# Layer normalisation by token tiles, and products ordered to match, in a two-layer hybrid decoder on one core

## The reference

```
h = layer_norm(x, emb_ln_g, emb_ln_b)
for i in range(2):
    mix = hybrid_mixer(h, ...)                      # projections, attention, linear recurrence, @ w_out
    h = layer_norm(ALPHA * h + mix, ln1_g[i], ln1_b[i])
    ffn = peer_ffn(h, ...)                          # 16384 experts, 16 of them per token and head
    ple = sigmoid(h @ ple_gate_w[i]) * (p[i] @ ple_w[i])
    h = layer_norm(ALPHA * h + ffn + ple, ln2_g[i], ln2_b[i])

def layer_norm(x, g, b):                            # over the 1024 columns of a token
    mu = x.mean(-1); var = square(x - mu).mean(-1)
    return (x - mu) * rsqrt(var + 1e-5) * g + b
```

## Time and profile before

| | |
|---|---|
| median of 3 runs | 3377.86 us (3376.49 to 3378.57) |
| the profiled execution | 3379.62 us, span from first to last instruction 3377.8 us |
| TensorE busy | 3236.6 us (96%) |
| VectorE busy | 2538.5 us (75%) |
| Pool busy | 2055.1 us (61%) |
| ScalarE busy | 1386.4 us (41%) |
| mean granted TensorE clock | 0.987 of full speed |

### The profile page before, as it was taken

How to read it: one execution, slowest core, us unless ns; L and a number is a source line. 1 busy time by engine, 2 the same in 40 slices (tenths; PEclk the granted TensorE clock), 3 DMA queues, 4 the chain that set the end, 5 groups by cost and what they waited for, 6 DMA issues and landing times. The chain is left out here.

```text
span 3377.8 us, 47082 instructions
## 1 busy us (share of the span) xinstructions
PE 3236.6 (96%) x17370; PEld 2888.0 (86%) x17370; DVE 2538.5 (75%) x4654; ACT 1386.4 (41%) x2726; POOL 2055.1 (61%) x1388
## 2 busy tenths in 40 slices
PE   5999899999999999999989998999999999999996
PEld 4787689999999988888777876899999999888885
DVE  5965359886876588888877734698769656888887
ACT  1235013466666533333212531135666664333331
POOL 5931677666677655555479046766666776555552
PEclk9999899999999999999999999999999999999998
DMA  3210224687899999999623012256888999999994
GB/s 122 89 68 26 88 75 159 230 294 298 298 334 355 354 387 370 360 361 363 245 75 99 32 51 88 76 200 239 302 301 300 348 352 357 384 364 361 359 362 154
DMA packets 312676, 817.12 MB, mean 242 GB/s; under 512 B 22272, under 2 KB 119552, under 8 KB 309120
## 3 DMA queue, kind: packets, MB, share of 16 engines
q1 hardware_dynamic: 112256, 349.02, 29.8%
q0 software_dynamic: 73728, 268.47, 20.6%
q10 hardware_dynamic: 126464, 196.63, 16.6%
HBM read 712.84 MB, written 101.19 MB: 241 GB/s over the span
## 5 line engine op out<-in xcount | busy, mean ns | idle before, releaser
L1247 POOL TENSOR_TENSOR u_lo<-panel,u_hi 128x1024 fp32r<-128x1024 f32 x256 | 619.4, 2420 | 318.0 <-ACT u_hi L1052 314.5
L594 PE MATMUL ps<-hT_hi,u_lo 128*128 128x384 f32 x2048 | 700.3, 342 | 0.0
L594 PE MATMUL ps<-hT_lo,u_hi 128*128 128x384 f32 x2048 | 684.6, 334 | 0.0
L594 PE MATMUL ps<-hT_hi,u_hi 128*128 128x384 f32 x2048 | 684.5, 334 | 0.0
L594 PE MATMUL ps<-v_hi,w_lo 128*128 128x512 f32 x1536 | 597.7, 389 | 0.1
L594 PE MATMUL ps<-v_hi,w_hi 128*128 128x512 f32 x1536 | 597.5, 389 | 0.0
L594 PE MATMUL ps<-v_lo,w_hi 128*128 128x512 f32 x1536 | 597.5, 389 | 0.0
L1264 POOL TENSOR_TENSOR v_lo<-panel,v_hi 128x1024 fp32r<-128x1024 f32 x128 | 311.6, 2434 | 381.7 <-ACT v_hi L1114 381.6
L1199 POOL TENSOR_TENSOR ring_hi<-panel,cst 128x512 fp32r<-128x512 f32 x244 | 275.4, 1129 | 432.1 <-PE ps L574 254.6
L1114 ACT CAST v_hi<-panel 128x1024 fp32r<-128x1024 f32 x256 | 269.1, 1052 | 641.8 <-PE ps L594 637.9
L1052 ACT CAST u_hi<-panel 128x1024 fp32r<-128x1024 f32 x256 | 268.1, 1048 | 445.4 <-PE ps L594 442.5
(11 more groups left out here) (264 smaller groups left out, 5670.1 us busy)
## 6 DMA issues: line engine op xcount, KB each, us to landing
panel<-in_u SPq DMA_DIRECT2D x256, 512.0 KB
panel<-in_v SPq DMA_DIRECT2D x256, 512.0 KB
gate_scratch<-arena ACTq DMA_DIRECT2D x24, 2048.0 KB
act_scratch<-arena ACTq DMA_DIRECT2D x124, 384.0 KB
arena<-act_scratch ACTq DMA_DIRECT2D x62, 768.0 KB
arena<-gate_scratch ACTq DMA_DIRECT2D x62, 768.0 KB
panel<-in_w_in SPq DMA_DIRECT2D x28, 1024.0 KB, 5.2
panel<-in_wq SPq DMA_DIRECT2D x16, 1024.0 KB, 5.1
```

What stands on the lines that cost most here:

```text
L594: mm = nc.tensor.matmul(o, lhs[a], rhs[b_], start=(start and n == 0), stop=(stop and n == 2))
L1247: pr.mark(nc.gpsimd.tensor_tensor(u_lo[:, j % URING].rearrange("p c n -> p (c n)"), u_tile(j), u_hi[:, j % URING].rearrange("p c n -> p (c ...
```

## The change

Both normalisations go token tile by token tile, and the products ahead of them finish token tile by token tile:

- `project` of the output's second half does its first four chunks as before and its last four (all that the ring holds) with the token tile as outer loop.
- The second expert product does tiles 0 to 123 as before and the last `GROUP` of four with the token tile as outer loop, signalling `y_tile` after each.
- VectorE takes moments of the first half early (`moments`), and then, for each token tile, adds, takes moments and makes the variance (`tile_variance`, `summed_variance`), with a root of its own on ScalarE. Scaling is two operations instead of three: (h - mean) * g, then * rstd + b (`tile_scaled`), in an order that puts other tiles' variances between.
- Token tile 0's moments and first scaling read `acc0` in PSUM; its copy to h is gone. `ADDED` reaches 128 at tile 123 instead of 127.
- Pool splits the query weights (panels 9 and on) only after all four tiles of the first normalisation; in layer 1 TensorE's first transposition also waits for all additions of the layer before.
- SP sends the output as four transfers, one for each token tile.

```diff
-ADDED = [max(0, (tile_ - LATE_DOTS) * SLOTS // (NK - 1 - LATE_DOTS)) for tile_ in range(NK)]
+ADDED = [min(SLOTS, max(0, (tile_ - LATE_DOTS) * SLOTS // (NK - 1 - GROUP - LATE_DOTS))) for tile_ in range(NK)]
...
-                    for c in range(NC):
+                    for c in range(NC - RING if tiles_last else NC):
...
+                    if tiles_last:
+                        late = []
+                        for m in range(4):
+                            for c in range(NC - RING, NC):
+                                if m == 0:
+                                    late.append(next_chunk())
+                                    used[0] += 1
+                                mm = matmul3(o4[m], [x_[:, c, m * P:(m + 1) * P] for x_ in (hT_hi, hT_lo)],
+                                             late[c - NC + RING], False, c == NC - 1)
+                                if m == 3:
+                                    pr.mark(mm, ring_used)
+                            if m < 3:
+                                pr.mark(mm, products)
+
+
+                if layer > 0:
+                    pe.wait_ge(y_added.sem, layer * y_added.per_layer)
                 turn(h, G_T1, 0, -NT)
...
+                for i in range(3):
+                    for j in range(NK - GROUP, NK):
+                        if i == 0:
+                            need_v_lo(pr, j)
+                            pe.wait_ge(w_lo_ready.sem, layer * w_lo_ready.per_layer + j + 1)
+                        for half in range(2):
+                            mm = second(j, i, half)
+                        if i == 2:
+                            pr.mark(mm, y_done)
+                    if i < 2:
+                        pr.mark(mm, y_tile)
...
-                root(3, rstd[:])
+                for i in range(NT):
+                    root(3 + i, rstd[:, i:i + 1])
...
-                split_panels(7, len(MIXER_PANELS), 1, 2)
+                split_panels(7, 9, 1, 2)
+                pool.wait_ge(h_ready.sem, layer * h_ready.per_layer + h_ready.before + NT)
+                split_panels(9, len(MIXER_PANELS), 1, 2)
...
+                def tile_variance(i):
+
+                    mixed(4 + i)
+                    step(moments(4 + i))
+                    variance(i)
+
+                def variance(i):
+
+                    step(nc.vector.bn_aggr(mv[:, i, :], stat[:, i, :]))
+                    pr.mark(nc.vector.tensor_scalar(rstd[:, i:i + 1], mv[:, i, 1:2], LN_EPS, None, ALU.add), var_ready)
+
+                def tile_scaled(i, roots, src=None):
+
+                    pr.need(root_ready, roots)
+                    step(nc.vector.reciprocal(rstd[:, i:i + 1], rstd[:, i:i + 1]))
+                    ins = nc.vector.scalar_tensor_tensor(out=h[:, i, :], in0=h[:, i, :] if src is None else src,
+                                                         scalar=mv[:, i, 0:1], in1=lng[:, 0, :],
+                                                         op0=ALU.subtract, op1=ALU.mult)
+                    if src is None:
+                        step(ins)
+                    else:
+                        pr.link(ins, y_added)
+                    pr.mark(nc.vector.scalar_tensor_tensor(out=h[:, i, :], in0=h[:, i, :], scalar=rstd[:, i:i + 1],
+                                                           in1=lng[:, 1, :], op0=ALU.mult, op1=ALU.add), h_ready)
...
+                tile_variance(0)
+                tile_scaled(0, 3)
+                tile_variance(1)
+                tile_variance(2)
+                tile_scaled(1, 4)
+                tile_variance(3)
+                tile_scaled(2, 5)
+                tile_scaled(3, 6)
...
-                pr.mark(nc.vector.tensor_copy(h[:, 0, :], acc0), y_added)
...
+                def summed_variance(i):
+
+                    if i < 3:
+                        dve.wait_ge(y_tile.sem, layer * y_tile.per_layer + i)
+                    else:
+                        dve.wait_ge(y_done.sem, layer * y_done.per_layer + NK)
+                    for half in range(2):
+                        hh = h[:, i, half * 512:(half + 1) * 512]
+                        n = pr.mark(nc.vector.tensor_tensor(hh, hh, bank(2 * (i - 1) + half), ALU.add), y_added)
+                    pr.need(y_added, n)
+                    for half in range(2):
+                        last = nc.vector.bn_stats(stat[:, i, 6 * half:6 * half + 6], h[:, i, half * 512:(half + 1) * 512])
+                    step(last)
+                    variance(i)
+
+                row_variance()
                 dve.wait_ge(ln2_in.sem, layer * ln2_in.per_layer + 32)
-                norm(h, step, root, lambda ins: pr.mark(ins, h_ready))
+                tile_scaled(0, 7, acc0)
+                summed_variance(1)
+                tile_scaled(1, 8)
+                summed_variance(2)
+                summed_variance(3)
+                tile_scaled(2, 9)
+                tile_scaled(3, 10)
...
-            sp.dma_start(out.rearrange("(i p) d -> p i d", p=P), h[:]).then_inc(out_sent.sem, 16)
-            sp.wait_ge(out_sent.sem, 16)
+            for i in range(NT):
+                sp.wait_ge(h_ready.sem, DEPTH * 2 * NT + i + 1)
+                sp.dma_start(out[i * P:(i + 1) * P, :], h[:, i, :]).then_inc(out_sent.sem, 16)
+            sp.wait_ge(out_sent.sem, 16 * NT)
```

More of the change, by code:

```diff
@@ L777, in _ @@
                 for half in range(2):
-                    project(lambda i: take(G_OUT + 4 * half + i, (pre1, 4 * half + i + 1)), True, None if half else 1)
+                    project(lambda i: take(G_OUT + 4 * half + i, (pre1, 4 * half + i + 1)), True, None if half else 1,
+                            half == 1)
                 turn(h, G_T3, 2, 0)
@@ L857, in _, with second @@
                 pe.wait_ge(g_kept.sem, layer * g_kept.per_layer + NG)
-                for j in range(NK):
+                def second(j, i, half):
+                    return matmul3(bank(2 * i + half), [x_[:, j % GROUP, i * P:(i + 1) * P] for x_ in (w_hi, w_lo)],
+                                   [x_[:, j % VRING, half * 512:(half + 1) * 512] for x_ in (v_hi, v_lo)],
+                                   j == 0, j == NK - 1)
+                for j in range(NK - GROUP):
                     need_v_lo(pr, j)
@@ L865, in _ @@
                                        + max(u for u in range(NK) if ABANKS[u % 3] == k) + 1)
-                        mm = matmul3(bank(k), [x_[:, j % GROUP, i * P:(i + 1) * P] for x_ in (w_hi, w_lo)],
-                                     [x_[:, j % VRING, half * 512:(half + 1) * 512] for x_ in (v_hi, v_lo)],
-                                     j == 0, j == NK - 1)
+                        mm = second(j, i, half)
                     pr.mark(mm, y_done)
+                for i in range(3):
[4 more added lines that the diff above has]
+                        for half in range(2):
+                            mm = second(j, i, half)
+                        if i == 2:
+                            pr.mark(mm, y_done)
+                    if i < 2:
+                        pr.mark(mm, y_tile)
         @block.scalar
@@ L1565, in _, with mixed @@
                 turn(G_T2, 1)
-                for g in range(8):
+                def mixed(g):
                     half, i = g // 4, g % 4
@@ L1571, in _, with moments @@
                                                            op0=ALU.mult, op1=ALU.add), pre1)
-                dve.wait_ge(pre1.sem, layer * pre1.per_layer + 8)
-                dve.wait_ge(ln1_in.sem, layer * ln1_in.per_layer + 32)
-                norm(h, step, root, lambda ins: pr.mark(ins, h_ready))
+                def moments(g):
+                    half, i = g // 4, g % 4
+                    dve.wait_ge(pre1.sem, layer * pre1.per_layer + g + 1)
+                    return nc.vector.bn_stats(stat[:, i, 6 * half:6 * half + 6], h[:, i, half * 512:(half + 1) * 512])
@@ new lines, in _ @@
+                for g in range(4):
+                    mixed(g)
+                for g in range(4):
+                    last = moments(g)
+                step(last)
+                dve.wait_ge(ln1_in.sem, layer * ln1_in.per_layer + 32)
+                tile_variance(0)
[6 more added lines that the diff above has]
+                tile_scaled(3, 6)
```

30 lines of the change are left out of this document (15 added, 15 removed).

## The result

The changed kernel takes 3341.68 us (median of 4 runs, 3339.52 to 3346.2) where the kernel before takes 3378.22: a ratio of 0.989 with a 95% interval of 0.9879 to 0.9902, 36.5 us less. Run again later beside the experiments it took 3341.83 against 3379.79, a ratio of 0.9886 (0.987 to 0.9903). The prediction was 3333.0 with a range of 3325 to 3344 and faster at 0.96: the sign and the range held, and 8.7 us of the gain forecast did not come. The narrower own range of the forecast, 3329 to 3341 with a chance of 0.70, was missed by 0.7 us.

A forecast was written before the change was run, and what follows sets the result against it. TensorE, at 96% of the span, was taken as the bound, so only its pauses at four serial normalisation stretches could be won. Gains of 17.1 + 12.3 + 15.9 = 45.3 us gave 3333, range 3325 to 3344.

The forecast's parts named there:

- the clock's level at the three restarts: TensorE's restarts behind the shortened pauses: up to 0.6 us each, allowed for in the own range only.
- (a): Rival, second product's last group later than thought: with 3 us more in each layer, 3339; chance 0.13.
- (b): Rival, Pool paces the query projection once its lead is gone: 5 us lost a layer, 3343; chance 0.08.
- First normalisation: Behind the output projection: last h 8.8 us earlier; gains 8.9 in layer 0 and 8.2 in layer 1, together 17.1.
- the split of chunk 7: Output projection's second half: Pool finishes this split later than wanted, stalling TensorE 0.54 us.
- Second normalisation: Behind the second expert product: gain on h 12.26 us, taken as 12.3 in layer 0; 15.9 in layer 1 with the store.
- The stall for w_lo of tile 126: Second product's last group: TensorE stalls 1.4 us for this late operand, covered by VectorE.
- second product longer than 524: Sign on the second expert product's duration: the prediction is wrong if it exceeds 524 us.
- Store: End of kernel: last of four output stores lands 3.0 us from issue, bounds 2.7 to 3.8, instead of 6.6; gain 3.6.
- (c): Rival, waiting is free on VectorE in the four normalisations: 7 us less, 3326; chance 0.05.
- (d): Rival, VectorE can't hold the second product with denser row sums: at 2.0 us a sum, 96 lost, 3429; chance 0.03.
- (e): Rival, no effect, tile order only moves VectorE's work about, its total behind TensorE remaining 22 us: 3378; chance 0.01.

The follow-up runs named there:

- e1: Changed kernel with idle transposes on TensorE in all three shortened pauses: 3334.68 us, ratio 0.9869 to the kernel before.
- e7: Changed kernel with idle transposes only in the two pauses ahead of the query projection, none ahead of layer 1's first projection: 3338.26 us, ratio 0.9875.
- e11: Changed kernel with all three pauses filled by idle transposes once more, timed beside the changed kernel: 3335.71 us, ratio 0.987 to the kernel before.
- e8: Kernel before the change with idle transposes in the two pauses ahead of the query projection: 3378.6 us, ratio 0.9993.
- e3: Changed kernel with both products in the old order, normalisations by tiles kept: 3358.21 us, ratio 0.9937 to the kernel before.
- e4: Kernel before with only the two-operation scaling, in all five normalisations including the embedding's: 3367.46 us, ratio 0.9964.
- e6: Changed kernel with the output in one transfer of 2 MB instead of four of 0.5 MB: 3345.21 us, ratio 0.9898 to the kernel before.
- e5: Changed kernel with the row sums (ADDED) as late as before the change: 3356.84 us, ratio 0.993 to the kernel before.
- e2: Changed kernel without Pool's wait for all of h ahead of splitting the query weights: 3344.99 us, ratio 0.9899 to the kernel before.
- e10: Changed kernel with three pauses filled, and Pool's first query split let go one token tile earlier: 3339.64 us, ratio 0.988 to the kernel before.

## Why the prediction was right, and what it missed

**The mis-sized term** is the clock's level at the three restarts. The prediction put it in the own range as "up to 0.6 each" and in the sum at nothing. It measured 2.3, 2.6 and 2.8 us, 7.7 in all, of a shortfall of 8.7. The 1 us left is a net: the four gains together came out 2.2 too small, and the rest of the kernel gave 1.2 back in the later execution. I took the level from the earlier trace rows, where one restart of the kernel before was slow for two matmuls and the others not at all, and didn't ask what the change does to the work that had brought the clock back. In the kernel before the transposes came in two blocks of 16, close to the projection; now they come as 16, 8 and 8 with waits for VectorE between, and TensorE restarts at the lower of its two levels. e1, e7 and e11 show that the clock's level is the cause of the loss, by taking it away where they fill; the three restarts of the kernel before, with none to two slow matmuls, and e8 show that it is new. That the thinner row of transposes is what brings the lower level about is argued, not shown: no run pairs the transposes again in the changed kernel. For it speaks that all 19 unfilled restarts in the traces of the changed kernel and its variants had 5 to 13 slow matmuls, behind pauses of 11.1 to 19.4 us, and all 7 of the old order none to two, behind 19.3 to 24.7. The length of the pause alone is not it: e3 had 7 or 8 behind 19.0 and 19.4 us, e4 at most one behind 19.3. In layer 1 the clock was back (the last 8 transposes took 1.09 us) and had fallen again by the restart 1.4 us later. The Trainium skill's page TensorE: Matmul & The Clock Gate, section What's actually happening, says that the clock follows how busy TensorE has lately been and that the number of slow matmuls varies between runs of one kernel. The rows agree with the first in the main, since filling brought the full clock back at 9 of 11 restarts, and with the second: two executions of the changed kernel had the same 13, 12 and 13, but the same restarts in e6 had 5, 8 and 12.

**Luck.** The full range held by 2.3 us, and not for its own reasons. It was widened for rivals (a) and (b), neither of which came; what used up the room was the clock, for which the prediction had allowed 1.8 us at most and which took 7.7.

**First normalisation.** 8.2 and 7.2 instead of 8.9 and 8.2. VectorE's chain is 18.3 us instead of 18.0 (one tile's aggregate takes 0.21 where the prediction had 0.16, four times), the wait for the split of chunk 7 costs 0.8 of TensorE's lead instead of 0.54, and the first addition starts 7.3 us ahead of the product's last matmul (2017.12, 2024.44) where I had 7.8. All three are small and on the same side. Pool's release at 2.57 and the lead growing from there were right: TensorE lost nothing to Pool further on.

**Second normalisation.** 11.9 for 12.3. The stall for w_lo of tile 126 came as computed, and VectorE covered it. My sign "second product longer than 524" was crossed by 0.25 (524.25): the stall cost TensorE 1.7 with the gaps around it. It was too tight a sign, since nothing hung on TensorE there. e5 shows that ending the row sums four tiles earlier is a real part of the gain, worth 6.5 a layer, more than the 5.1 that four sums take.

**Store.** 2.6 instead of 3.0, just outside my lower bound, hidden in the end stage by 0.5 more of VectorE.

**The rivals.** (a) The last group was not late beyond the stall. (b) Pool didn't pace the projection, but the mutual slowing that it built on is real where VectorE is busy, as e2 and e10 show. (c) Waiting is not free: an operation that waits still starts 0.04 behind the end of the one before (3321.40 after 3321.20 + 0.16). (d) Row sums stayed at 1.28. (e) is excluded by the result.

**Still open.** What decides how many matmuls a restart runs at the lower level, 5 to 13 behind equal pauses, isn't shown, nor why one filled restart of e10 was slow. In layer 1 between the query projection's restart and the last group of the second product the first profiled execution lost 1.2 us, where the second one gained 0.3; no run was made for it. Whether fewer idle transposes would do was not tried.

## What to carry to other kernels

Shortening a pause of TensorE is worth its length less what the clock takes back at the restart. List the work that TensorE does inside the pause, before and after, and if it is thinned out, price the restart by rows at the lower level or fill the pause with idle work, which helped at most restarts here, not at all of them. Where VectorE and Pool both read two inputs from SBUF, order them one behind the other on the path that sets the end, even if Pool then starts late. A filler between two waits (here a row sum) is worth more than its own duration once it is moved out.

## What the runs showed of the hardware

- Behind a pause of 11 to 13 us with 32 transposes as 16, 8 and 8, TensorE ran 5 to 13 matmuls of 512 columns at 1.2 GHz (12 or 13 in two executions of the changed kernel, 5, 8 and 12 in e6); behind one of 19 to 25 us with the same 32 in two blocks, none to two. The longer pause had the quicker restart. The number differs between executions of the same instructions.
- A VectorE scaling with two inputs in SBUF takes 1.28 us alone and mostly 2.0 to 2.2 beside Pool's splits, which go from 1.04 or 1.28 to 2.0 or 2.1; whichever starts first keeps its own time.
- A store of 0.5 MB lands in 2.6 us, one of 2 MB in 6.6: 4.0 us for 1.5 MB more.
